# A transformer layer pair in fp32 on one core: the third branch's projection in chunk order ahead of its gates, weights through three staging buffers, four buffers handed to expert weights

## The chip, the core and the metric

The kernel runs on one core of a Trainium2 chip. The metric is the device time of one launch in microseconds; lower is better. Before the change it is 2053.32 us, the median of three runs.

## What is computed

Two blocks in fp32 on 256 tokens of width 1024. The part that the change touches is the end of the first block's mixer and the beginning of its mixture of experts:

```python
merged = (jax.nn.sigmoid(ga) * (o_a @ w_branch_a)
          + jax.nn.sigmoid(gb) * (o_b @ w_branch_b)
          + jax.nn.sigmoid(gc) * (o_c @ w_branch_c))   # gc, ga, gb: 1024 columns of h @ w_in
x = x + gt1 * (merged @ w_out)
h2 = rmsnorm(x, norm2_g) * (1.0 + sc2) + sh2
x = x + gt2 * hier_moe(h2, rg_w, rg_b, re_w, re_b, e_gate, e_up, e_down)
```

`o_a` and `o_b` have 1024 columns, `o_c` has 2048, so `w_branch_c` is 2048 x 1024 (8 MB) and the others are half of that. The experts are 32, each with three matrices of 2 MB: 201 MB that are all read, since tokens choose their two experts by data. After the experts come the second block's feed-forward layers, a gated mixer and an attention.

## The kernel before

**Engines and staging.** TensorE (PE) multiplies in fp32 by splitting each weight into a rounded high part H and a remainder L: `three` (L650 to L653) issues H times high, H times low and L times high of the other operand. SyncE (SP) issues nearly all loads. A load of 1 MB goes into one of five raw buffers (`NR` = 5, tiles m_49 to m_53 in the order rows), and feeds two *pieces* of 1024 columns. ScalarE (ACT) rounds a piece to H (L1597), VectorE (DVE) subtracts to get L (L2304); both sit in one of four piece slots (`NH` = 4). So ACT may make the piece that is four further on only when PE has used the present one, and a raw buffer is free when DVE has made the L of its second piece. ACT, DVE and SP each keep the order of `plan`: whatever stands in between waits its turn, and what stands behind waits with it. `ahead(p)` on each of them works up to piece p + 3.

**Branches.** For A, B and C the code loops over four groups of 256 columns: the gate (`Cg0` and so on, 2 pieces, moving operand hT) and the projection (`Cw0`, for C 4 pieces of 8 row chunks by 128 columns, moving operand ocT, the turned `o_c`). A piece is 24 matmuls. PE accumulates in PSUM: kind "m" goes round banks 0 to 3, kind "s" round banks 4 to 7, and `take` waits until the bank's last contents have been read. ACT makes the sigmoid of the gate in the buffer `gs` (L1806), DVE multiplies it by the projection (L2560), GpSimd (POOL) adds the product to `mg` (L3351), and for the last step ACT rounds `mg` to mgT high (`mg_high`, L1820) and DVE makes its low part (`mg_low`, L2580). In C the projection of a group is taken out in two halves of 256 columns, each with its own product and sum.

**Output projection.** `w_out` (pieces of `wo`: 2 chunks of rows by 512 columns, for both halves of the tokens) reads mgT. Its pieces 0 and 1 are multiplied as they come; piece 2 is held until piece 3 is there, so PE waits for the L of piece 3 before it goes on with piece 2. DVE multiplies by gt1 and adds to x (L3156, L3159), then comes the router, which ends in the logits `lg`, and the gather of tokens for the experts.

**Where expert weights go.** Each 1 MB half of an expert matrix has a place in a table (`by_half` in `plan_experts`): the raw buffers, places `ex` 0 to 10 and `pre` 0 to 6, which are stretches of memory that earlier tensors use. SP fetches into a place as soon as its last reader is done; this is written by hand in `sync` (L3432 and L3518 on): `ex` 0 to 4, 9 and 10 and `pre` 4 during branch C, `pre` 1, 0, 2 and the raw buffers around its end, `ex` 5 to 8 as `w_out` gives up the piece slots, and `pre` 5, 6 and 3 when the logits are complete. From then on a place is filled again when the experts' matmuls (L1115, L1126) have read it. `pre` 5 is the memory of the first half of ocT high (35360 on), `pre` 1 that of the first half of ocT low (39456 on), `pre` 0 that of the 2048 columns from 37408. The scratch buffers `wos`, `rj` and `rF[0]` of `w_out` and the router lie in `pre` 5.

## Time and profile before

| | |
|---|---|
| median of 3 runs | 2053.32 us (2052.53 to 2053.99) |
| profiled execution, its own time | 2053.77 us |
| its span, first to last instruction | 2051.9 us |
| PE busy | 1908.7 us, 93% |
| DVE busy | 1133.1 us, 55% |
| ACT busy | 903.5 us, 44% |
| mean granted TensorE clock | 0.97 |
| HBM read | 500.07 MB, 244 GB/s over the span |

The page divides the span into 40 slices of 51.3 us. Times in the rows below are microseconds from the span's start. PEld is the loading of weights into TensorE, SPq the queue from which SyncE issues DMAs. In the timeline a row is: start, duration, engine, line, operation, result<-inputs, shapes, number of instructions merged, and in brackets the idle time before it and what ended it. Matmul durations overlap, so that a matmul's price is the distance of two starts.

### The profile page before, as it was taken

What the parts mean: (1) busy time and instruction counts of PE and PEld (TensorE: products, weight loads), DVE (VectorE), ACT (ScalarE), POOL (GpSimd) and SP (SyncE); (2) the same over time, 40 slices, a digit from 0 to 9 for tenths busy, and PEclk for the clock granted to TensorE, in tenths of its full rate; (3) what the DMA queues carried; (4) which work ended last, traced back from release to release, by engine and by line L of the source; (5) the groups of instructions that cost most, each with busy time, mean ns of one, the idle gap of its engine ahead of it and who ended that gap; (6) DMA issues with size and microseconds to landing.
All of it is one profiled execution on the core that took longest, in us unless ns stands there. A gap on an engine that the chain in (4) does not pass through costs nothing.

```text
span 2051.9 us, 30543 instructions
## 1 busy us (share of the span) xinstructions
PE 1908.7 (93%) x12777; PEld 1485.8 (72%) x12777; DVE 1133.1 (55%) x1523; ACT 903.5 (44%) x1289; POOL 118.8 (6%) x101
## 2 busy tenths in 40 slices
PE   9999999999999866766699999999999999999998
PEld 7899988889984211111178888888888888988887
DVE  3678876678542110101156666756667666756666
ACT  4655555544342100000045555545456554675544
POOL 0244331001000000000000000000000000000000
PEclk9999999999999988788899999999999999999999
DMA  9654546788899999999985755545554555525552
GB/s 349 211 159 153 164 145 226 231 269 283 288 354 410 424 426 425 426 425 424 421 290 192 243 190 184 166 164 175 192 188 163 186 190 192 174 85 172 188 185 83
DMA packets 241761, 503.51 MB, mean 245 GB/s; under 512 B 11457, under 2 KB 165714, under 8 KB 222418
## 3 DMA queue, kind: packets, MB, share of 16 engines
q1 hardware_dynamic: 240720, 500.70, 67.8%
q8 instruction: 103, 1.69, 0.3%
q10 hardware_dynamic: 898, 0.80, 0.1%
q14 instruction: 40, 0.33, 0.0%
HBM read 500.07 MB, written 1.07 MB: 244 GB/s over the span
## 4 chain that ended last, share of the span: by engine, by line
PE 73%; DMA 14%; DVE 7%; ACT 3%; issue 2%; SPq 1%; POOL 0%; ACTq 0%; DVEq 0%
PE bank L651 14%; PE bank L712 14%; PE bank L653 13%; PE bank L652 13%; PE bank L714 7%; DMA m<-in_expert_w_up 4%; DMA m<-in_expert_w_down 4%; DMA m<-in_expert_w_gate 4%; PE bank L1115 3%; DVE m L2304 2%; PE bank L1126 2%; ACT m L1597 1%; PE bank L996 1%; SPq L3414 1%; DMA m<-in_ffn_w_in 0%
## 5 line engine op out<-in xcount | busy, mean ns | idle before, releaser
L2304 DVE TENSOR_TENSOR m<-m,m 128x1024 fp32r<-128x1024 f32 x505 | 625.7, 1254 | 287.0 <-ACT m L1597 284.8
L651 PE MATMUL bank<-m,m 128*128 128x256 f32 (+1 forms) x1960 | 658.4, 336 | 6.6 <-DVE m L2304 3.0
L653 PE MATMUL bank<-m,m 128*128 128x256 f32 (+1 forms) x1960 | 645.6, 329 | 0.0
L652 PE MATMUL bank<-m,m 128*128 128x256 f32 (+1 forms) x1960 | 645.2, 329 | 0.0
L1597 ACT ACTIVATE m<-m 128x1024 fp32r<-128x1024 f32 x505 | 524.2, 1054 | 223.1 <-PE bank L653 203.9
L712 PE MATMUL bank<-m,m 128*128 128x512 f32 x1248 | 439.8, 394 | 0.0
L651 PEld LDWEIGHTS bank<-m,m 128*128 128x128 f32 x1960 | 368.6, 188 | 55.7 <-DVE m L2304 10.0
L653 PEld LDWEIGHTS bank<-m,m 128*128 128x128 f32 x1960 | 368.6, 188 | 36.5
L652 PEld LDWEIGHTS bank<-m,m 128*128 128x128 f32 x1960 | 368.9, 188 | 33.8 <-issue 1.2
L714 PE MATMUL bank<-m,m 128*128 128x256 f32 x1248 | 352.7, 283 | 0.0
L712 PEld LDWEIGHTS bank<-m,m 128*128 128x128 f32 x1248 | 234.4, 188 | 54.0
L714 PEld LDWEIGHTS bank<-m,m 128*128 128x128 f32 x1248 | 234.6, 188 | 1.6
L1115 PE MATMUL bank<-m,m 128*32 128x512 f32 x1024 | 163.7, 674 | 59.8 <-DMA m<-in_expert_w_gate 33.3
L1115 PEld LDWEIGHTS bank<-m,m 128*32 128x32 f32 x1024 | 39.7, 121 | 175.3 <-issue 85.6
L1948 ACT ACTIVATE m<-bank 128x256 f32<-128x256 f32 x156 | 59.2, 379 | 161.5 <-PE bank L714 161.5
L1126 PE MATMUL bank<-m,m 128*32 128x512 f32 x512 | 91.3, 679 | 36.6 <-DMA m<-in_expert_w_down 30.8
L2855 DVE TENSOR_TENSOR m<-bank,m 128x256 f32<-128x256 f32 x156 | 65.6, 422 | 59.6 <-ACT m L1948 54.9
L1126 PEld LDWEIGHTS bank<-m,m 128*32 128x32 f32 x512 | 19.2, 122 | 101.1 <-DMA m<-in_expert_w_down 56.5
L2730 DVE TENSOR_TENSOR m<-bank,m 128x512 f32<-128x512 f32 x16 | 10.3, 686 | 142.1 <-PE bank L1126 142.1
L2724 DVE SCALAR_TENSOR_TENSOR m<-bank,m,m 128x512 f32<-128x512 f32 x8 | 6.0, 750 | 118.3 <-PE bank L1115 118.3
L2751 DVE TENSOR_TENSOR m<-m,bank 128x512 f32<-128x512 f32 x32 | 21.3, 686 | 87.1 <-PE bank L1198 87.1
L1859 ACT ACTIVATE m<-bank 128x512 f32<-128x512 f32 x8 | 4.8, 597 | 133.0 <-PE bank L1115 133.0
(352 smaller groups left out, 1384.1 us busy)
## 6 DMA issues: line engine op xcount, KB each, us to landing
m<-in_ffn_w_in SPq DMA_DIRECT2D x88, 1024.0 KB, 5.1
m<-in_w_in SPq DMA_DIRECT2D x60, 1024.0 KB, 5.2
m<-in_ffn_w_out SPq DMA_DIRECT2D x44, 1024.0 KB, 5.0
m<-in_expert_w_up SPq DMA_DIRECT2D x40, 1024.0 KB, 21.8
m<-in_expert_w_down SPq DMA_DIRECT2D x34, 1024.0 KB, 18.0
m<-in_expert_w_gate SPq DMA_DIRECT2D x33, 1024.0 KB, 22.8
m<-in_expert_w_gate SPq DMA_DIRECT2D x15, 2048.0 KB, 23.4
m<-in_expert_w_down SPq DMA_DIRECT2D x13, 2048.0 KB, 17.9
```

What stands on the lines that cost most here:

```text
L651: e.matmul(o, s[0], m[0], start=first, stop=False, skip_group_check=skip)
L652: e.matmul(o, s[0], m[1], start=False, stop=False, skip_group_check=skip)
L653: return e.matmul(o, s[1], m[0], start=False, stop=last, skip_group_check=skip)
L712: e.matmul(b[:, :].rearrange("p (h n) -> p h n", h=2), H, N.both[:, k], start=k == 0, stop=False, skip_group_check=True)
L714: ins = e.matmul(b[:, 0:256], L, N.T[0][:, k, :], start=False, stop=k == 7, skip_group_check=True)
L1115: ins = e.matmul(b[32 * j:32 * j + 32, :], XG(q, q + 1)[:, 0, k, 32 * j:32 * j + 32], block(ld, i), start=k == 0, stop=k == 7, skip_group_ ...
L1126: ins = e.matmul(b[n][32 * j:32 * j + 32, :], eT[q % 2][:, 128 * c + 32 * j:128 * c + 32 * j + 32], ld.raw[:, 1024 * i + 512 * n:1024 * i ...
L1597: inc(e.activation(rv(fit(q.H, q.view.shape)), q.view, ACT.Copy), "h", skey(q, "H"))
L1948: inc(e.activation(fb[6][:, 256 * b:256 * b + 256], k[:, 256:512], ACT.Copy), "ffn", (f"f{z}c", n, c, b))
L2304: inc(e.tensor_tensor(rv(fit(q.L, q.view.shape)), q.view, fit(q.H, q.view.shape), ALU.subtract), "l", skey(q, "L"))
L2751: taken(e.tensor_tensor(o, o if q else x[:, t, 512 * n:512 * n + 512], b[:, :], ALU.add), "ey", q, t, n, also=[("y", q, t, n)])
L2855: taken(e.tensor_tensor(o, k[:, 0:256], fb[6][:, 256 * b:256 * b + 256], ALU.add), f"f{n}{z}{c}", b, also=[(f"f{z}a", n, c, b)])
```

## The change

It touches branch C and its surroundings in each engine's program; what is computed stays the same.

1. The projection of C no longer goes group by group. `plan_third` takes `w_branch_c` in loads of 4 row chunks by 512 columns, first all columns of rows 0 to 511, then the next 512 rows, and so on, into four banks (0 to 3), one for each group of 256 columns. Seven of its eight loads (`Ca`, 14 pieces) come first, then the four gates (8 pieces, in banks 4 to 7), then the last load (`Cz`, 2 pieces, groups 2 and 3).
2. From branch C on, up to the end of `w_out`, weights go round three raw buffers (m_51, m_52, m_53). The other two (m_49, m_50) take expert weights when B's last weights have been split.
3. `pre` 5 and `pre` 1 are fetched when piece 7 of `Ca` is used (the first eight chunks of ocT are then read). `wos`, `rj` and `rF[0]` move by 2048 columns into `pre` 0, which is now fetched with `pre` 6 and 3 after the logits.
4. `gs` has two buffers for C (the second is B's). Products and sums are made over 512 columns at a time, once a group. `mg_high` and `mg_low` of groups 0 and 1 stand ahead of `Cz`, those of 2 and 3 behind it.

```diff
@@ -213,13 +213,13 @@
         plan, G = [], {}
         tails, counts = {}, {}
         loads, XL, OL = [], {}, {}
+        ring = list(range(NR))
 
         def load(dst, src, slot=None, release=None):
             if slot is None:
-                kind, n = "raw", NR
-                c = counts.get(kind, 0)
-                counts[kind] = c + 1
-                slot = (kind, c % n)
+                c = counts.get("raw", 0)
+                counts["raw"] = c + 1
+                slot = ("raw", ring[c % len(ring)])
...
+        def plan_third(gcol, W):
+            G["Ca"], G["Cz"] = [], []
+            for k0 in (0, 4, 8, 12):
+                for h in range(2):
+                    last = k0 == 12 and h == 1
+                    for i in range(4 if last else 0):
+                        plan_gemm2(f"Cg{i}", win, 8, [gcol + 256 * i])
+                    ld = load(lambda r: r.rearrange("p (k n) -> p k n", n=512),
+                              W[128 * k0:128 * k0 + 512, 512 * h:512 * h + 512].rearrange("(k p) n -> p k n", p=128))
+                    v = ld.raw.rearrange("p (k n) -> p k n", n=512)
+                    for i in range(2):
+                        G["Cz" if last else "Ca"].append(Piece(plan, ld, v[:, :, 256 * i:256 * i + 256], 1024, name="Cw",
+                                                               g=2 * h + i, k=k0, m=4, end=k0 == 12))
...
+        ring[:] = [(counts["raw"] + i) % NR for i in range(3)]
+        counts["raw"] = 0
+        plan_third(GC, a["w_branch_c"][0])
         plan_gemm1("wo", a["w_out"][0], 8, 0, 1024)
         plan_experts()
         plan_overflow()
-        counts["raw"] = 0
+        ring[:], counts["raw"] = range(NR), 0
...
-        gs = {"A": mem(37152, 512), "B": mem(44064, 512), "C": mem(43552, 512)}
+        gs = {"A": mem(37152, 512), "B": mem(44064, 512), "C": [mem(43552, 512), mem(44064, 512)]}
-        wos = mem(36384, 512)
-        rj = mem(36896, 512)
-        rF = [v256(mem(o, 1024)) for o in (35360, 44576)]
+        wos = mem(38432, 512)
+        rj = mem(38944, 512)
+        rF = [v256(mem(o, 1024)) for o in (37408, 44576)]
...
+            def products(name):
+
+                for p in walk(name):
+                    w.wait_ge(*skey(p, "L"))
+                    o = take(p.g, "Cw", p.g) if p.k == 0 else bank[p.g]
+                    for b in range(2):
+                        for i in range(4):
+                            k = p.k + i
+                            w.wait_ge("ocT", k // 2)
+                            ins = three(o[:, 256 * b:256 * b + 256], parts(p, 256 * i + 128 * b, 128),
+                                        (ocT[0][:, k, :], ocT[1][:, k, :]), k == 0 and b == 0, k == 15, True)
+                    used(ins, p, *([("Cw", p.g)] if p.end else []))
+
+            def third_branch():
+                products("Ca")
+                for i in range(4):
+                    if i == 1:
+                        router_bias()
+                    gemm2(f"Cg{i}", hT, h_ready, at="s")
+                    if i < 2:
                         ada_sum(10 + i)
+                products("Cz")
+                turn["m"] = 0
...
+            def third_branch():
+                run("Ca")
+                for i in range(4):
+                    def ev_gate(p):
+                        b = got(p.name, p.g)
+                        if i >= 2:
+                            w.wait_ge("bs", "C", i - 2)
+                        elif i:
+                            w.wait_ge("bs", "B", 3)
+                        else:
+                            w.wait_ge("full", ("ada", 5))
+                        taken(e.activation(gs["C"][i % 2], b[:, :], ACT.Sigmoid), p.name, p.g, also=[("bg_s", "C", i)])
+                    run(f"Cg{i}", ev_gate)
+                e.activation(eps[:, 2:3], eps[:, 0:1], ACT.Sqrt)
+                mg_high(0)
+                mg_high(1)
+                run("Cz")
+                mg_high(2)
+                mg_high(3)
...
+            def third_branch():
+                def ev_out(i):
+                    b = got("Cw", i)
+                    s = gs["C"][i % 2]
+                    w.wait_ge("bg_s", "C", i)
+                    taken(e.tensor_tensor(s, s, b[:, :], ALU.mult), "Cw", i, also=[("bsv", "C", i)])
+                for n, p in enumerate(walk("Ca")):
+                    if n == 4:
                         router_weights()
-                    run(f"{name}g{i}")
-                    if name == "C" and i == 3:
-                        for j in range(3):
-                            mg_low(j)
-                    run(f"{name}w{i}", ev_out)
-                    if name != "C":
-                        run_ada(*adas[name][i])
-                    elif i < 2:
+                for i in range(4):
+                    run(f"Cg{i}")
+                    if i < 2:
+                        ev_out(i)
                         ada_out(10 + i)
-                    if name == "C" and i == 2:
+                    if i == 1:
                         b = got("rbias")
                         taken(e.tensor_tensor(rt["bias"], b[:, 0:36], rB, ALU.add), "rbias")
+                mg_low(0)
+                mg_low(1)
+                run("Cz", lambda p: ev_out(p.g))
+                mg_low(2)
+                mg_low(3)
...
+            def third_branch():
+                for n, p in enumerate(G["Ca"]):
+                    ahead(p)
+                    if n == 2:
                         w.wait_ge("full", ("ocT", 7))
                         w.wait_ge(*skey(G["Bw3"][-1], "used"))
-                        for slot in ((0, 1), (2, 3))[i]:
+                        w.wait_ge("taken", ("cd", 3))
+                        for slot in (0, 1):
                             fetch(first("ex", slot))
-                        if i == 0:
-                            w.wait_ge("taken", ("cd", 3))
-                            fetch(first("ex", 4))
+                    if n == 5:
+                        for slot in (2, 3):
+                            fetch(first("ex", slot))
+                    if n == 8:
+                        fetch(first("ex", 4))
+                    if n == 10:
+                        w.wait_ge(*skey(G["Ca"][7], "used"))
+                        for slot in (5, 1):
+                            fetch(first("pre", slot))
+                run("Cg0", "Cg1")
+                w.wait_ge("taken", ("rbias",))
+                fetch(first("ex", 10))
+                run("Cg2", "Cg3")
+                w.wait_ge(*skey(G["Cg3"][-1], "used"))
+                fetch(first("pre", 4))
+                run("Cz")
...
-            w.wait_ge(*skey(G["Cw3"][-1], "used"))
-            for i in (0, 2):
-                fetch(first("pre", i))
+            w.wait_ge(*skey(G["Cz"][-1], "used"))
+            fetch(first("pre", 2))
...
-            for i in (5, 6, 3):
+            for i in (6, 0, 3):
```

Three places show how the order of instructions moves. Names like m_51 are buffers. The first is SyncE's queue from the first load of `w_out` to the first refill of an expert place. Before:

```order
L3414 DMA m_53<-in_w_out 128x4x512 [waits dve_l]
...
L3414 DMA m_82<-in_expert_w_up 128x2048 [waits used]
L3414 DMA m_49<-in_expert_w_up 128x2048 [waits dve_l]
L3414 DMA m_81<-in_expert_w_up 128x2048 [waits used]
L3414 DMA m_83<-in_expert_w_up 128x2048
L3414 DMA m_50<-in_expert_w_up 128x2048 [waits dve_l]
L3414 DMA m_51<-in_expert_w_down 128x2048 [waits dve_l]
L3414 DMA m_78<-in_expert_w_down 128x2048 [waits used]
...
L3414 DMA m_86<-in_expert_w_gate 128x2048 [waits full4]
L3412 DMA m_87<-in_expert_w_gate 128x1024
...
L3414 DMA m_84<-in_expert_w_up 128x2048
L3414 DMA m_68<-in_expert_w_down 128x2048 [waits ex_used]
```

After:

```order
L3463 DMA m_51<-in_w_out 128x4x512 [waits dve_l]
...
L3463 DMA m_52<-in_expert_w_down 128x2048 [waits dve_l]
L3463 DMA m_83<-in_expert_w_up 128x2048 [waits used]
L3463 DMA m_53<-in_expert_w_down 128x2048 [waits dve_l]
L3463 DMA m_51<-in_expert_w_down 128x2048 [waits dve_l]
L3463 DMA m_78<-in_expert_w_down 128x2048 [waits used]
...
L3461 DMA m_87<-in_expert_w_gate 128x1024 [waits full4]
...
L3463 DMA m_81<-in_expert_w_up 128x2048
L3463 DMA m_84<-in_expert_w_up 128x2048
L3463 DMA m_68<-in_expert_w_down 128x2048 [waits ex_used]
```

Four loads of expert weights (into m_49, m_50, m_82 = `pre` 1 and m_86 = `pre` 5) have moved up to a place ahead of the first load of `w_out`; m_81 = `pre` 0 has moved back to the place that `pre` 5 had. In all, from the first load of branch C to the one before the last `m_51<-in_expert_w_down`, there are 30 loads of 1 MB in either order.

The second is TensorE's queue where branch B ends and C begins. Before:

```order
L651 MATMUL bank0<-m133_181,m6_54 128x256
L652 MATMUL bank0<-m134_182,m6_54 128x256
L653 MATMUL bank0<-m133_181,m10_58 128x256
L651 MATMUL bank1<-m83_131,m7_55 128x256 [waits bank1_act,dve_l]
L652 MATMUL bank1<-m84_132,m7_55 128x256
```

After:

```order
L667 MATMUL bank0<-m134_182,m6_54 128x256
L668 MATMUL bank0<-m135_183,m6_54 128x256
L669 MATMUL bank0<-m134_182,m10_58 128x256
L667 MATMUL bank0<-m137_185,m7_55 128x256 [waits bank0_dve,dve_l]
L668 MATMUL bank0<-m138_186,m7_55 128x256
```

The last projection of B is in bank 0. What follows it went to bank 1 before; now it goes to bank 0 and waits for DVE's read of it (`bank0_dve`).

The third is VectorE's queue around the last pieces of branch C. m139/m140 is mgT low, m132 and m133 are `gs` of C, lines L2304/L2351 the subtractions of weights. Before:

```order
L2580 TENSOR_TENSOR m139_187<-m124_172,m138_186 128x512 [waits act_split] x3
...
L2304 TENSOR_TENSOR m12_60<-m5_53,m8_56 128x1024 [waits used,act_h]
L2560 TENSOR_TENSOR m132_180<-m132_180,bank3 128x256 [waits bank2_act,used]
L2304 TENSOR_TENSOR m13_61<-m1_49,m9_57 128x1024 [waits act_h]
L2560 TENSOR_TENSOR m132_180<-m132_180,bank0 128x256 [waits used]
L2580 TENSOR_TENSOR m139_187<-m124_172,m138_186 128x512 [waits act_split]
L2304 TENSOR_TENSOR m10_58<-m1_49,m6_54 128x1024 [waits act_h]
```

After:

```order
L2635 TENSOR_TENSOR m140_188<-m124_172,m139_187 128x512 [waits act_split] x2
L2351 TENSOR_TENSOR m12_60<-m3_51,m8_56 128x1024 [waits used,act_h]
L2613 TENSOR_TENSOR m132_180<-m132_180,bank2 128x512 [waits bank7_act,used]
L2351 TENSOR_TENSOR m13_61<-m4_52,m9_57 128x1024 [waits act_h]
L2613 TENSOR_TENSOR m133_181<-m133_181,bank3 128x512 [waits bank4_act,used]
L2635 TENSOR_TENSOR m140_188<-m124_172,m139_187 128x512 [waits act_split] x2
L2351 TENSOR_TENSOR m10_58<-m4_52,m6_54 128x1024 [waits act_h]
```

The last row of each is the L of `w_out`'s piece 3. Ahead of it stand now two products of 512 columns and two of `mg_low`, where two products of 256 and one `mg_low` stood.

## Rows read from the trace of the kernel before

**Rows 1.** The page: span, and GB/s in 40 slices of it

```profile
span 2051.9 us, 30543 instructions
...
GB/s 349 211 159 153 164 145 226 231 269 283 288 354 410 424 426 425 426 425 424 421 290 192 243 190 184 166 164 175 192 188 163 186 190 192 174 85 172 188 185 83
```

**Rows 2.** Stretches: us, busy PE, PEld, DVE, ACT, POOL, PEclk, DMA share, GB/s

```profile
585.00:595.00 10.00, 10.00 (x45) 8.10 (x44) 6.25 (x7) 4.09 (x7) 0.00 (x0) 1.00 0.96 404
595.00:597.00 2.00, 2.00 (x15) 1.74 (x14) 0.02 (x1) 0.94 (x2) 0.00 (x0) 1.00 0.47 82
597.00:605.00 8.00, 7.63 (x130) 6.16 (x129) 2.92 (x5) 2.95 (x8) 0.00 (x0) 1.00 0.99 394
605.00:616.00 11.00, 10.33 (x154) 7.18 (x153) 4.58 (x27) 5.04 (x5) 0.00 (x0) 1.00 1.02 410
616.00:620.00 4.00, 4.00 (x40) 2.45 (x42) 1.26 (x6) 2.21 (x5) 0.00 (x0) 1.00 0.85 310
...
660.00:1060.00 400.00, 284.38 (x1569) 88.50 (x1562) 53.53 (x80) 31.60 (x58) 0.00 (x0) 0.85 1.01 420
```

**Rows 3.** Timeline of SyncE's queue, 570 to 620 us

```profile
576.05 11.08 SPq L3414 DMA_DIRECT2D m<-in_expert_w_up  x5
595.04 7.82 SPq L3414 DMA_DIRECT2D m<-in_expert_w_down  x5
...
615.80 0.33 SPq L3414 DMA_DIRECT2D m<-in_expert_w_down  x1
```

**Rows 4.** Timeline of TensorE, end of branch B and beginning of C

```profile
507.61 0.28 PE L653 MATMUL bank<-m,m 128*128 128x256 f32 x1
507.73 0.28 PE L651 MATMUL bank<-m,m 128*128 128x256 f32 x1
```

**Rows 5.** Timeline of VectorE, the product of B's last group

```profile
507.93 0.69 DVE L2560 TENSOR_TENSOR m<-m,bank 128x512 f32<-128x512 f32 x1 [1.75 <-PE bank L653]
```

**Rows 6.** Timeline of ScalarE, last gate and last pieces of branch C

```profile
567.50 0.60 ACT L1806 ACTIVATE m<-bank 128x512 f32<-128x512 f32 x1 [1.73 <-PE bank L653]
...
569.52 1.66 ACT L1820 ACTIVATE m<-m 128x512 fp32r<-128x512 f32 x3
571.08 3.17 ACT L1597 ACTIVATE m<-m 128x1024 fp32r<-128x1024 f32 x3
576.11 1.06 ACT L1597 ACTIVATE m<-m 128x1024 fp32r<-128x1024 f32 x1 [1.85 <-PE bank L653]
580.16 0.63 ACT L1820 ACTIVATE m<-m 128x512 fp32r<-128x512 f32 x1 [2.99 <-POOL m L3351]
```

**Rows 7.** Timeline of VectorE, end of branch C

```profile
576.04 0.42 DVE L2560 TENSOR_TENSOR m<-m,bank 128x256 f32<-128x256 f32 x1 [0.39 <-PE bank L653]
...
578.89 0.42 DVE L2560 TENSOR_TENSOR m<-m,bank 128x256 f32<-128x256 f32 x1 [0.47 <-PE bank L653]
580.83 0.69 DVE L2580 TENSOR_TENSOR m<-m,m 128x512 fp32r<-128x512 f32 x1 [1.51 <-ACT m L1820]
581.78 2.36 DVE L2304 TENSOR_TENSOR m<-m,m 128x1024 fp32r<-128x1024 f32 x2 [0.26 <-ACT m L1597]
```

**Rows 8.** Timeline of TensorE, first matmul of `w_out` and of its piece 2

```profile
578.70 0.39 PE L651 MATMUL bank<-m,m 128*128 128x512 f32 x1
...
584.27 0.39 PE L651 MATMUL bank<-m,m 128*128 128x512 f32 x1
```

**Rows 9.** Timeline of GpSimd: sums over 512 columns in B, 256 in C

```profile
472.32 1.30 POOL L3351 TENSOR_TENSOR m<-m,m 128x512 f32<-128x512 f32 x1 [120.73 <-DVE m L2560]
485.91 2.20 POOL L3351 TENSOR_TENSOR m<-m,m 128x512 f32<-128x512 f32 x1 [12.29 <-DVE m L2560]
...
579.39 0.73 POOL L3351 TENSOR_TENSOR m<-m,m 128x256 f32<-128x256 f32 x1 [2.11 <-DVE m L2560]
```

**Rows 10.** Timeline of VectorE around the second of these sums

```profile
485.75 3.44 DVE L2304 TENSOR_TENSOR m<-m,m 128x1024 fp32r<-128x1024 f32 x2
```

**Rows 11.** Loads of w_branch_c: issue to landing

```profile
DMA to landing us min/median/max: 5.2/7.0/10.0
```

More of the change, by code:

```diff
@@ L579, in build @@
         rt["pr"] = tmp(64).rearrange("p (t e g) -> p t g e", t=2, g=4)
-        adas = {"A": later[4:8], "B": later[12:16], "C": []}
+        adas = {"A": later[4:8], "B": later[12:16]}
         def reach(p):
@@ L1520, in tensor @@
             ticks.join()
-            branch("C", ocT, lambda k: ("ocT", k // 2), 16)
+            third_branch()
             w_out()
@@ L1803, in ev_gate @@
                             w.wait_ge("oaL", 1)
-                        elif name == "C":
-                            w.wait_ge("full", ("ada", 5))
                         taken(e.activation(gs[name], b[:, :], ACT.Sigmoid), p.name, p.g, also=[("bg_s", name, i)])
                     run(f"{name}g{i}", ev_gate)
-                    if name == "C" and i == 3:
-                        e.activation(eps[:, 2:3], eps[:, 0:1], ACT.Sqrt)
-                        for j in range(3):
-                            mg_high(j)
                     run(f"{name}w{i}")
-                    if name != "C":
-                        run(("ada", *adas[name][i]))
+                    run(("ada", *adas[name][i]))
+            def third_branch():
[17 more added lines that the diff above has]
+                mg_high(3)
             def mg_high(j):
                 w.wait_ge(*skey(G["Cg3"][-1], "used"))
-                w.wait_ge("mg", "C", j, 1)
+                w.wait_ge("mg", "C", j, 0)
                 o = slice(512 * j, 512 * j + 512)
@@ L2172, in scalar @@
             ticks.join()
-            branch("C")
-            mg_high(3)
+            third_branch()
             def x_copy(g, t):
@@ L2547, in ev_out @@
                     def ev_out(p):
[L2548 to L2552 removed]
+                        b = got(p.name, 0)
+                        s = gs[name]
                         w.wait_ge("bg_s", name, i)
@@ L3147, in vector @@
             ticks.join()
-            branch("C")
-            mg_low(3)
+            third_branch()
             def ev_wo(p):
@@ L3434, in branch @@
                     run(f"{name}g{i}")
-                    if name == "C" and i == 3:
-                        w.wait_ge("taken", ("rbias",))
-                        fetch(first("ex", 10))
-                        w.wait_ge(*skey(G["Cg3"][-1], "used"))
-                        fetch(first("pre", 4))
-                        for p in G["Cw3"][:3]:
-                            ahead(p)
-                        w.wait_ge(*skey(G["Cw3"][1], "used"))
-                        fetch(first("pre", 1))
                     run(f"{name}w{i}")
-                    if name != "C":
-                        run(("ada", *adas[name][i]))
+                    run(("ada", *adas[name][i]))
                     if name == "A" and i == 1:
@@ L3517, in sync @@
             branch("B")
-            branch("C")
+            third_branch()
             ahead(G["wo"][0])
-            w.wait_ge(*skey(G["Cw3"][-1], "used"))
-            for i in (0, 2):
-                fetch(first("pre", i))
+            w.wait_ge(*skey(G["Cz"][-1], "used"))
+            fetch(first("pre", 2))
             run("wo")
```

39 lines of the change are left out of this document (11 added, 28 removed).

## Prediction

> **What bounds the kernel now.** I read the page first, then stretches around the end of the first block, then the timelines of the engines there. The page's row of bytes [rows 1] has a plateau of 410 to 426 GB/s from the 13th slice to the 20th, from 616 us to 1026; before it the rate is 145 to 354. The long stretch 660 to 1060 says the same: the DMA engines are busy all the time (share 1.01) at 420 GB/s, while PE has work for 284 of 400 us [rows 2]. So the experts are bound by loads, and what lies ahead of them is bound by PE: in 585 to 597 it is busy in every microsecond [rows 2], and the matmuls of branch C follow each other at 0.12 us [rows 4].
>
> The change is meant to load expert weights earlier, so the question is what the loads wait for where the plateau begins. From 585 to 595 the share is 0.96; then, in 595 to 597, it falls to 0.47 with 82 GB/s; from 597 on it is 0.99 and over 1 [rows 2]. SyncE's queue explains the hole: the five loads of `in_expert_w_down` begin to be issued at 595.04 [rows 3]. They wait for the piece slots and the raw buffer that `w_out` gives up, that is for PE. At that moment all earlier loads have landed, or the rate could not fall to 82. After the five come the three places that wait for the logits, and at 615.80 the first refill, which waits for the experts' first matmuls [rows 3].
>
> This gives the rule I forecast by: **what has been moved by 595, and when PE gets there, set the end of the experts.** In the two orders of SyncE's queue, 30 loads of 1 MB stand between the start of branch C and that hole, before and after; behind it stand the same waits, with `pre` 0 where `pre` 5 was. Four expert loads go earlier, but the loads that they overtake were in by 595 too. Nothing is gained: the DMA engines will only be busier before 585 and idle longer before 595. What is left is the path of PE.
>
> **The change on PE's path.** Its work stays: 24 pieces of 24 matmuls of one shape, two sums for the modulation, one for the router's bias. A piece takes 578.89 - 576.04 = 2.85 us, the distance of the two products that wait for the ends of two pieces [rows 7]. Cost 0.
>
> *Loads through three buffers.* A raw buffer is free when the L of its second piece, p, is made, and this begins when PE has used piece p - 4. The next load in the buffer holds piece p + 5, and ACT may begin on that when PE has used p + 1. Between the two ends lie 5 pieces, 14.2 us. H and L take about 2.6 us of them before the issue (1.06 + 1.22 and what separates them [rows 6, 7]); 11.6 us are left until the split would be late. PE would be late about 6 us after that: it has three more pieces, 8.5 us, less 2.3 for H and L. Landing took 5.2 to 10.0 us for these loads [rows 11]. Two expert loads may now stand ahead, each 1.05 MB at 420 GB/s = 2.5 us [rows 2], so up to 15 us. That is below 11.6 + 6.2 = 17.8. I take 0; the cover is this lead, and without it each late load costs its excess.
>
> *A wait at the start of C.* PE's order shows that the first piece of `Ca` writes bank 0, in which B's last projection has just been finished, and waits for DVE to read it. Before, the next bank was free and PE went on from 507.61 to 507.73 [rows 4]. The read runs from 507.93 for 0.69 us, to 508.62 [rows 5]. An engine follows another's end in about 0.05 us (POOL's sum ends at 580.12, ACT starts at 580.16, ends at 580.79, and DVE starts at 580.83 [rows 6, 7, 9]). So PE goes on at 508.67: **0.94 us lost**. Bounds 0.9 and 1.1; there is no other work for PE, whose queue keeps its order.
>
> *A wait in w_out.* I write W for `w_out`'s first matmul, 578.70 before; its piece 2 starts at W + 5.57 [rows 8]. PE needs the L of piece 3 by then. Before it was made at 581.78 + 1.22 = 583.00, W + 4.3, 1.3 us early (the pair took 2.36, and one subtraction takes 1.22) [rows 7]. After the change the gates end later: there are two pieces between the last gate and W, where there were four. So, in order:
> - ACT's last sigmoid moves from 567.50 to two pieces later, W - 5.50. As before it takes 2.02 us until `mg_high` and 0.52 for each of now two: ACT is free at W - 2.44 [rows 6]. Two roundings of 1.06 follow. DVE subtracts (`wo` 1) from W - 1.34 to - 0.12, so its product of group 2, ready since W - 2.66, is late: W - 0.20 to 0.49. Then comes the subtraction for `wo` 2, 0.40 to 1.62, and the product of group 3, 1.54 to 2.23.
> - POOL's sum over 512 columns took 1.30 us where DVE ran no subtraction, 2.20 where it began in one; that pair of subtractions then took 3.44 instead of 2.36 [rows 7, 9, 10]. Group 2's sum begins in a subtraction: 0.57 to 2.77. Group 3's does not: 2.81 to 4.11.
> - `mg_high` of group 3 starts at W + 4.15. From its start to the end of L of piece 3 it was 583.00 - 580.16 = 2.84 [rows 6, 7], so L ends at W + 6.99 and PE goes on at 7.04: **1.5 us lost**.
>
> Bounds for the second: both sums at 1.30 give W + 6.55, 1.0 us; both at 2.20 give 7.95, 2.4 us. I take the middle since each sum is nearest to its own row of the two.
>
> On the second and third of these steps the Trainium skill has a rule, "SBUF — State Buffer", section "Who interferes with whom": a DVE instruction with two SBUF inputs and a GpSimd instruction that reads SBUF hold a shared read port exclusively, and the second fully blocks. By that rule, which the 3.44 us bear out, the 0.9 us are waiting for the subtraction and not slower adding, so group 3's sum costs 1.30 and the loss is 1.5; if sums next to any DVE work cost 2.20, it is 2.4.
>
> *Everything behind* hangs on PE: the L of `wo`'s pieces 4 and 5 are needed only 5.6 us later, the last five loads, the logits, the refill. The hole at 595 opens later by the whole sum, and behind it the plateau has the same bytes to move. `mg_low` and products over 512 instead of 256 columns hide in DVE's idle time (0.39 to 1.51 us ahead of each row [rows 7]) but for what is counted. The scratch that moved into `pre` 0 costs nothing: `pre` 0 is filled in the third of the loads after the logits, and is read only for the second half of the first experts' matrices.
>
> **Sum:** 0.94 + 1.5 = 2.4 us later. The profiled execution would go from 2053.77 to 2056.2; it stood 0.45 above the median, so against the median it is 2053.3 + 2.4 = **2055.8 us**, rounded up, 0.12% slower. A measurement of this kernel tells about 0.2%, 4.1 us, from no change: this is within it.
>
> **The rivals.**
> - *The two waits are hidden.* If DVE's order or POOL's timing is kinder than I walk it, the time stays at 2053 to 2054.5. For it: the second wait has 1.3 us of slack before. Against it: the bank wait is plain in the order. Chance 0.13.
> - *The ring starves PE*, the one that ends on the other side. Its place is the loads of `Ca` and of the gates behind the pairs `ex` 0/1, 2/3 and `pre` 5/1. It decides from landings over 17.8 us after the freeing. With 10.0 us for a landing and each pair 5 us, it needs 3 us more, from SyncE being held up at one of its hand-written waits. Each of three places would then cost one expert load, 2.5 us: 7.5 us on top, 2063. One such place gives 2058.3. Chance 0.13 for over 2057.4, with the bound of 2.4 us and other late splits among them.
> - *Early loads pay.* If some of the plateau's idle time is really owed to these four loads (the share is 0.85 in 616 to 620 [rows 2]), they take up to 4 x 2.5 = 10 us off: 2045.8. Against it stand the hole at 595 and the equal counts. The Trainium skill, "DMA: Bandwidth & Descriptors", section "Rules for kernel authors", advises to issue the DMA early and wait on it late; by it the change is right, but the rows say that the queue ran dry after these loads anyway. Chance 0.04.
> - *It does not do what it says*: a raw place is released as late as before. The order shows m_49 and m_50 filled ahead of `w_out`, so I give it nothing of its own.
>
> **How the numbers follow.** My case has 0.70 and spans 2054.8 to 2057.3 (bounds 0.9 + 1.0 and 1.1 + 2.4, and half a microsecond of scatter). Down to 2053.0 and up to 2058.6, the range takes in most of the hidden case and one starved load, and leaves out some 0.15. Faster by over 0.2% (below 2049.2): 0.04. Slower by over 0.2% (above 2057.4): 0.14. The rest, 0.82, is the same.
>
> **What would show it.** After the change: PE idle for about 0.9 us before `Ca`, put down to DVE's product; PE idle about 1.5 us inside `w_out`, put down to DVE's subtraction; GB/s higher in 500 to 560 and a share well under 0.96 before the hole, with the five loads issued about 2.4 us later than 595.04; the plateau as long as before, its end 2.4 us later. I am wrong if the queue is still loaded when these five are issued, or if PE waits in branch C.

## The result and the profile after

The changed kernel took 2055.77 us (median of 20 runs, 2053.80 to 2056.95). The kernel before, run beside it, took 2052.68 us (20 runs, 2051.39 to 2053.99). The ratio is 1.0014, with a 95% interval of 1.0008 to 1.0020: slower by 3.1 us, inside the 0.2% that the prediction called "the same", and within its range. The profiled execution took 2055.20 us, with a span of 2053.4. Of all runs in this document one is left out, of the kernel called *one held* below: it took 3694.9 us.

The page of the changed kernel, span and GB/s in 40 slices (to set beside [rows 1]):

```profile
span 2053.4 us, 30540 instructions
...
GB/s 349 210 163 149 165 144 227 232 270 280 327 295 413 425 427 423 427 424 425 420 302 188 243 190 185 168 164 172 193 190 164 186 188 192 175 86 172 187 184 83
```

Stretches of it: us, busy PE, PEld, DVE, ACT, POOL, PEclk, DMA share, GB/s (to set beside [rows 2], moved by the delay):

```profile
500.00:560.00 60.00, 59.13 (x546) 58.15 (x544) 32.73 (x35) 22.52 (x23) 3.49 (x2) 1.00 0.91 327
560.00:585.00 25.00, 25.00 (x188) 23.61 (x187) 14.20 (x16) 12.36 (x17) 4.73 (x3) 1.00 0.71 251
585.00:589.00 4.00, 2.77 (x13) 1.97 (x12) 3.74 (x4) 2.59 (x3) 0.00 (x0) 1.00 0.26 39
589.00:593.00 4.00, 4.00 (x19) 3.25 (x18) 0.55 (x2) 1.15 (x2) 0.00 (x0) 1.00 1.00 424
597.00:599.00 2.00, 2.00 (x14) 1.69 (x13) 0.89 (x1) 0.58 (x3) 0.00 (x0) 1.00 0.19 29
599.00:605.00 6.00, 6.00 (x31) 4.91 (x29) 1.45 (x3) 1.74 (x4) 0.00 (x0) 1.00 0.96 370
...
660.00:1060.00 400.00, 286.90 (x1568) 88.66 (x1568) 53.83 (x81) 30.91 (x55) 0.00 (x0) 0.83 1.01 421
```

Two of the same stretches of the kernel before:

```profile
500.00:560.00 60.00, 60.00 (x554) 58.72 (x553) 34.31 (x40) 24.04 (x25) 5.69 (x6) 1.00 0.86 297
560.00:585.00 25.00, 25.00 (x187) 23.82 (x187) 14.71 (x17) 13.04 (x17) 2.40 (x4) 1.00 0.81 299
```

The early loads do come early: from 500 to 560 the rate rises from 297 to 327 GB/s. It is paid back from 560 to 585 (299 to 251), and just before the last loads of this stage the queue now runs dry at 585 to 589 (39 GB/s); the kernel before had a shallower place of this kind a little earlier, 123 GB/s at 582 to 585. The hole is still there: 29 GB/s at 597 to 599, in place of 82 at 595 to 597. From 660 to 1060 the plateau is as before, 421 GB/s. SyncE's queue, timeline (to set beside [rows 3]):

```profile
586.99 0.34 SPq L3463 DMA_DIRECT2D m<-in_expert_w_down  x1
587.37 0.43 SPq L3463 DMA_DIRECT2D m<-in_expert_w_up  x1
589.25 16.49 SPq L3463 DMA_DIRECT2D m<-in_expert_w_down  x6
...
618.68 0.33 SPq L3463 DMA_DIRECT2D m<-in_expert_w_down  x1
```

The row of six merges two things: a load for a raw buffer at 589.25, and the five loads that stood at 595.04 before, which are issued from 597.92 on. The first refill is issued at 618.68 where it was 615.80. Both are 2.9 us later, by the profile's own zero.

Where PE lost it, timeline of TensorE: the starts of branch C and of `w_out`'s piece 2 (to set beside [rows 4, 8]):

```profile
507.37 0.28 PE L669 MATMUL bank<-m,m 128*128 128x256 f32 x1
508.52 0.36 PE L667 MATMUL bank<-m,m 128*128 128x256 f32 x1 [0.87 <-DVE m L2603]
508.71 0.28 PE L668 MATMUL bank<-m,m 128*128 128x256 f32 x1
...
580.09 0.39 PE L667 MATMUL bank<-m,m 128*128 128x512 f32 x1
...
585.43 0.40 PE L669 MATMUL bank<-m,m 128*128 128x512 f32 x1
587.06 0.47 PE L667 MATMUL bank<-m,m 128*128 128x512 f32 x1 [1.23 <-DVE m L2351]
587.37 0.39 PE L668 MATMUL bank<-m,m 128*128 128x512 f32 x1
```

VectorE, timeline: B's last product, then the products of groups 2 and 3 with a subtraction of weights between them, `mg_low` twice, and three subtractions, the first of which makes the L of `w_out`'s piece 3 (to set beside [rows 5, 7]):

```profile
507.68 0.69 DVE L2603 TENSOR_TENSOR m<-m,bank 128x512 f32<-128x512 f32 x1 [1.76 <-PE bank L669]
...
579.87 0.68 DVE L2613 TENSOR_TENSOR m<-m,bank 128x512 f32<-128x512 f32 x1
580.46 1.22 DVE L2351 TENSOR_TENSOR m<-m,m 128x1024 fp32r<-128x1024 f32 x1
581.60 0.68 DVE L2613 TENSOR_TENSOR m<-m,bank 128x512 f32<-128x512 f32 x1
583.53 1.95 DVE L2635 TENSOR_TENSOR m<-m,m 128x512 fp32r<-128x512 f32 x2 [1.25 <-ACT m L1868]
585.73 3.50 DVE L2351 TENSOR_TENSOR m<-m,m 128x1024 fp32r<-128x1024 f32 x3 [0.26 <-ACT m L1632]
```

GpSimd and then ScalarE, timeline: the sums of groups 2 and 3 into `mg`, `mg_high` twice, and the roundings behind (to set beside [rows 6, 9]):

```profile
580.63 3.46 POOL L3404 TENSOR_TENSOR m<-m,m 128x512 f32<-128x512 f32 x2 [15.62 <-DVE m L2613]
```

```profile
582.86 0.63 ACT L1868 ACTIVATE m<-m 128x512 fp32r<-128x512 f32 x1 [3.22 <-POOL m L3404]
584.11 0.64 ACT L1868 ACTIVATE m<-m 128x512 fp32r<-128x512 f32 x1 [0.62 <-POOL m L3404]
584.65 2.94 ACT L1632 ACTIVATE m<-m 128x1024 fp32r<-128x1024 f32 x3
```

With W = 580.09 the walk of the prediction can be laid beside the rows: product of group 2 at W - 0.22 (foreseen - 0.20), product of group 3 at W + 1.51 (1.54), the sums from W + 0.54 to 4.00 (0.57 to 4.11), `mg_high` of group 3 at W + 4.02 (4.15), L of piece 3 done at 585.73 + 1.22, W + 6.86 (6.99).

### The profile page after: what moved, and what is told of

Its sections match the earlier page's. It is cut to its first block, busy times and chain, and to the rows that moved or that the text cites. A ratio compares the mean times of both kernels' runs of the same rounds, so it can differ in the third digit from the quotient of the medians.

```text
span 2053.4 us, 30540 instructions
## 1 busy us (share of the span) xinstructions
PE 1911.3 (93%) x12777; PEld 1487.0 (72%) x12777; DVE 1134.2 (55%) x1519; ACT 903.3 (44%) x1289; POOL 119.1 (6%) x97
## 3 DMA queue, kind: packets, MB, share of 16 engines
q8 instruction: 103, 1.69, 0.3%
## 4 chain that ended last, share of the span: by engine, by line
PE 75%; DMA 11%; DVE 7%; ACT 3%; issue 2%; SPq 1%; POOL 0%; ACTq 0%; DVEq 0%
PE bank L667 14%; PE bank L728 13%; PE bank L669 13%; PE bank L668 13%; PE bank L730 7%; DMA m<-in_expert_w_down 5%; DMA m<-in_expert_w_up 4%; PE bank L1150 3%; DMA m<-in_expert_w_gate 3%; PE bank L1161 2%; DVE m L2351 2%; PE bank L1031 1%; ACT m L1632 1%; SPq L3463 1%; DVE m L2469 0%
## 5 line engine op out<-in xcount | busy, mean ns | idle before, releaser
L2351 DVE TENSOR_TENSOR m<-m,m 128x1024 fp32r<-128x1024 f32 x505 | 627.3, 1257 | 291.0 <-ACT m L1632 288.9
```

The costliest lines, as they stand in the source:

```text
L2351: inc(e.tensor_tensor(rv(fit(q.L, q.view.shape)), q.view, fit(q.H, q.view.shape), ALU.subtract), "l", skey(q, "L"))
```

## Three stretches to measure by

The times of 11 runs leave an interval of about 0.0009 of 2053 us, 1.8 us, to either side. That is too wide to tell 1 us from 0. The distances in the trace vary less, if two things that differ from one execution to the next are left out: where in the span branch C begins (506.75 to 507.93 in the profiles of this study), and the experts' stretch behind. So each kernel is read by three rows: **P**, VectorE's product of B's last group (as [rows 5]); **W**, `w_out`'s first matmul (as [rows 8]); **R**, the first refill in SyncE's queue (as [rows 3]). P to W is branch C, W to R is `w_out` and the path to the experts. For the kernel before they are 507.93, 578.70, 615.80; changed 507.68, 580.09, 618.68.

| kernel | P to W | W to R | P to R, against before | median less the median of before, us | ratio, 95% interval |
|---|---|---|---|---|---|
| before | 70.77 | 37.10 | | | |
| changed | 72.41 | 38.59 | +3.13 | +3.09 | 1.0008 to 1.0020 |
| changed, again | 71.90 | 38.64 | +2.67 | +3.38 | 1.0006 to 1.0025 |
| bank turned | 70.78 | 38.58 | +1.49 | +1.69 | 0.9998 to 1.0016 |
| split first | 72.40 | 37.31 | +1.84 | +2.00 | 1.0002 to 1.0020 |
| both | 70.78 | 37.30 | +0.21 | +0.83 | 0.9993 to 1.0011 |
| both, again | 70.96 | 37.26 | +0.35 | +0.67 | 0.9995 to 1.0012 |
| wait in before | 71.88 | 37.11 | +1.12 | +1.50 | 0.9999 to 1.0018 |
| late four | 71.89 | 38.64 | +2.66 | +3.18 | 1.0008 to 1.0026 |
| ring of five | 71.90 | 38.64 | +2.67 | +3.56 | 1.0008 to 1.0026 |
| ring of two | 71.89 | 38.95 | +2.97 | +3.01 | 1.0004 to 1.0022 |
| one held | 71.87 | 38.60 | +2.60 | +4.35 | 1.0012 to 1.0029 |
| both and half | 70.78 | 37.30 | +0.21 | -0.92 | 0.9989 to 1.0007 |
| both and half, again | 70.96 | 37.26 | +0.35 | -0.15 | 0.9991 to 1.0008 |

The theory to test is the prediction's: PE lost its time at two waits, and neither the three buffers nor the early loads cost or gain anything. Its rivals: the three buffers or their transfers cost the time; or the early loads pay and hide a larger loss. One thing more was to be settled: in the changed kernel's profile P to W was 1.64 longer, and the bank wait explains 1.1 of it. The rest is a cadence, by which I mean the mean distance of two matmuls' starts: from 508 to 555 PE's matmuls of 256 columns started 120.0 ns apart (means over each 5 us of the timeline), everywhere around it 118.7.

## The experiments

**The changed kernel again**, as yardstick.

> The changed kernel once more, as the yardstick of the runs beside it. All theories: 2.5 to 3.5 us over the kernel before (2055.2 to 2056.2 if that one runs at 2052.7).

2056.19 us, 3.4 over the kernel before. Its branch C was half a microsecond shorter, 71.90, and the cadence was 118.7 throughout. So the 0.5 us of the first profile come and go in the same kernel.

**The projection in other banks.**

```diff
-                    o = take(p.g, "Cw", p.g) if p.k == 0 else bank[p.g]
+                    o = take((p.g + 1) % 4, "Cw", p.g) if p.k == 0 else bank[(p.g + 1) % 4]
...
-                turn["m"] = 0
+                turn["m"] = 1
```

> The projection's four sums stand in the banks 1, 2, 3, 0 in place of 0, 1, 2, 3, so that the first one no longer meets the bank that VectorE has yet to read. Theory of TensorE's path: the gap of 1.15 us ahead of the branch shrinks to 0.12, which gives back 1.0 us against the changed kernel. On the slower cadence (120.0 ns a matmul in the first part of the branch, 118.7 elsewhere) the two explanations part: if the stall sets it, the 120.0 goes with the stall, another 0.5 us, 1.5 in all; if the chunk order itself (its banks, weights or the split ahead) sets it, it stays, and only 1.0 is gained. Theory that the lost time is the three staging buffers' or the transfers': no gain from this, 0.0, since the loads stay as they are.

2054.50 us. TensorE's timeline, the same seam:

```profile
507.61 0.28 PE L669 MATMUL bank<-m,m 128*128 128x256 f32 x1
507.72 0.28 PE L667 MATMUL bank<-m,m 128*128 128x256 f32 x1
```

The gap is gone and P to W is back at 70.78. Against the second profile of the changed kernel, with the same cadence, that is 1.12 us; W to R is unchanged. The median fell 1.7 us against the changed kernel beside it; that is 0.6 more than the trace explains, and less than the interval of 1.8 us.

**The split of `w_out`'s piece 3 ahead of the last slices** of the merged activations. On ScalarE and on VectorE, before `mg_high(2)` and before `mg_low(2)`:

```diff
+                ahead_to(G["wo"][0].j + NH)
```

> ScalarE and VectorE make the halves of w_out's third piece ahead of the last two slices of the merged activations, not behind them; nothing else changes. Theory of TensorE's path: the gap of 1.63 us inside w_out is what VectorE's late half causes, so it goes and 1.2 to 1.4 us come back, unless the group of w_out that wants the last slices comes so early that they are late now: then less than 0.7. Theory of the three buffers or the transfers: 0.0. Theory that the early expert loads pay and cover a larger loss: 1.4 or more.

2054.81 us. TensorE's timeline at the start of `w_out`'s piece 2:

```profile
584.84 0.40 PE L669 MATMUL bank<-m,m 128*128 128x512 f32 x1
585.18 0.47 PE L667 MATMUL bank<-m,m 128*128 128x512 f32 x1
```

W to R falls from 38.59 and 38.64 to 37.31, by 1.3 us; 0.2 of the 1.5 stay. They stand in the same place: the step into piece 2 is 0.34 where it was 0.23 in the kernel before, and the next matmul starts 0.31 later and not 0.23. This profile has the slow cadence in branch C again (72.40), which is why P to R stands at +1.84. VectorE's timeline, then GpSimd's, show what the sums cost now:

```profile
581.61 1.72 DVE L2352 TENSOR_TENSOR m<-m,m 128x1024 fp32r<-128x1024 f32 x1
```

```profile
580.04 4.44 POOL L3406 TENSOR_TENSOR m<-m,m 128x512 f32<-128x512 f32 x2 [15.61 <-DVE m L2614]
```

With one more subtraction beside the second sum, the two sums take 4.44 us in place of 3.46, and the subtraction 1.72 in place of 1.22. It does no harm, since `mg_high` of group 3 is now needed last.

**Both edits**, run twice.

> The two edits together. Theory of TensorE's path: the gains add up, 2.4 us without the cadence and 2.9 with it, so the kernel stands within 0.5 us of the kernel before (2052.3 to 2053.3 against 2052.7), although its three staging buffers and early expert loads are those of the changed kernel. Theory of the three buffers or the transfers: it stays 2 to 3 us over the kernel before. Theory that the early loads pay: it falls more than 1 us below the kernel before.

> The two edits together, once more beside the next kernel. Theory of TensorE's path: 2.4 to 2.9 us under the changed kernel, 2052.5 to 2053.7, and within 0.8 us of the kernel before.

2053.64 and 2053.88 us, 0.8 and 0.7 over the kernel before, within the interval of no difference. Against the changed kernel the first is 2.6 us lower, as expected; 0.8 over the kernel before is more than the 0.5 that the first expectation allowed, and 2053.88 is 0.2 above the second's bound. P to R is +0.21 and +0.35 (in the second, with matmuls of 120.0 ns from 560 to 580). The gains add up in P to R, with three buffers and early loads in place. The rival that blames buffers or transfers said 2 to 3 us over the kernel before, and the one in which early loads pay said more than 1 us under it; neither came.

**The bank wait alone, in the kernel before.**

```diff
             ticks.join()
+            turn["m"] -= 1
             branch("C", ocT, lambda k: ("ocT", k // 2), 16)
```

> The kernel before with one thing more: the branch's first product goes to the bank that VectorE has not read yet, as in the change; order and buffers are those of before. Theory of TensorE's path: a gap of 1.1 us where there was 0.12, so 1.0 us slower than the kernel before. On the cadence: if the stall sets it, matmuls from there to the next change of shape (the small product for the adaptive weights at about 525) run at 120.0 in place of 118.7 ns, about 0.2 us more; if the chunk order sets it, 118.7 all through. If the wait were hidden: 0.0.

TensorE's timeline, the same seam:

```profile
506.43 0.28 PE L653 MATMUL bank<-m,m 128*128 128x256 f32 x1
507.58 0.36 PE L651 MATMUL bank<-m,m 128*128 128x256 f32 x1 [0.87 <-DVE m L2561]
507.77 0.28 PE L652 MATMUL bank<-m,m 128*128 128x256 f32 x1
```

2054.33 us, P to W 71.88: the wait costs 1.11 us, the same as in the changed kernel, and W to R stays at 37.11. The rows say how 1.11 comes about. The gap is 1.15 where it was 0.12, 1.03 more, and the matmul behind the first one starts 0.19 later and not 0.12. The cadence after this wait was 118.7.

**Four early loads late again.** In SyncE's queue the two raw places are filled behind the fetch of `ex` 10, which waits for the router's bias, and `pre` 5 and 1 with `pre` 4 behind `Cg3`. (The expectation counts five; `pre` 4 stood there already, so four have moved.)

```diff
                     if q.load.final is q and q.load.succ and q.load.succ.n not in fetched:
+                        if q.j < G["Ca"][0].j and q.load.succ.release:
+                            held.append(q.load.succ)
+                            fetched.add(q.load.succ.n)
+                            continue
                         fetch(q.load.succ)
...
                     if n == 10:
                         w.wait_ge(*skey(G["Ca"][7], "used"))
-                        for slot in (5, 1):
-                            fetch(first("pre", slot))
+                        pass
...
                 fetch(first("ex", 10))
+                for ld in held:
+                    fetch(ld)
...
-                fetch(first("pre", 4))
+                for slot in (4, 5, 1):
+                    fetch(first("pre", slot))
```

> The changed kernel with five of its early expert loads (two into staging buffers, three into the experts' own) issued late, after the second gate of the branch and after the fourth; all else as changed. Theory that the early loads gain nothing because all of them are in before the queue drains: as the changed kernel, within 0.3 us, with the same stretch of plateau after the first refill. Theory that the early loads pay: 1 us or more slower than the changed kernel. Theory that they do harm beside the branch (a load in the way of another, or the slower cadence of 120.0 ns from the heavier traffic between 500 and 560): 0.5 us or more faster, with a cadence of 118.7.

Stretches of this kernel, columns as above:

```profile
500.00:560.00 60.00, 59.13 (x549) 58.15 (x549) 32.59 (x35) 23.12 (x23) 3.48 (x2) 1.00 0.73 257
560.00:585.00 25.00, 24.65 (x180) 22.77 (x178) 14.58 (x17) 12.93 (x17) 4.74 (x3) 1.00 0.93 364
```

The rate of 500 to 560 falls from 327 to 257 GB/s: 70 GB/s over 60 us are 4.2 MB, four loads. The time is 2056.01 us, P to R +2.66, both as in the changed kernel, and the last load of an expert weight is issued 407.5 us after the first refill, in the changed kernel's two profiles 406.5 and 407.3. So taking these four loads early neither gains nor harms. That the cadence was 118.7 here says nothing of their traffic, since the changed kernel, run again, had 118.7 with that traffic.

**Five staging buffers, and two.**

```diff
-        ring[:] = [(counts["raw"] + i) % NR for i in range(3)]
+        ring[:] = [(counts["raw"] + i) % NR for i in range(NR)]
```

and `range(2)` for two.

> The branch's weights go round five staging buffers again, the new order stays, and the first expert loads into the two buffers more come late. Theory of TensorE's path: as the changed kernel, within 0.3 us. Theory of the three buffers: 1.5 to 3 us faster, the gap inside w_out smaller, since pieces come earlier. Theory that early loads pay: 1 us or more slower.

> The branch's weights go round two staging buffers in place of three. Theory of TensorE's path, by the buffer's cycle: a piece's buffer comes free one piece earlier than its use allows for, the load takes 5.2 to 10.0 us, and the lead of 11.6 us of three buffers falls by a third or more; at 7.8 us or less some loads come late and VectorE and ScalarE with them, TensorE waits 0 to 8 us in the branch, and the kernel is 0 to 8 us slower than the changed one. Theory that three buffers already cost 1.5 us or more: two cost at least twice that. 0.0 to 0.3 means the ring is wide enough even at two.

2056.39 and 2056.22 us. With five, both stretches are those of three to 0.01, and the median, 3.6 over the kernel before, lies 0.2 to 0.5 above the changed kernel's two, within the scatter. The rival of the three buffers said 1.5 to 3 us faster, the one of early loads 1 us or more slower. With two, P to W is unchanged, although the branch's last load is issued ten microseconds later; SyncE's timeline of the changed kernel, then of the ring of two:

```profile
551.46 0.38 SPq L3463 DMA_DIRECT2D m<-in_w_branch_c  x1
```

```profile
561.58 0.37 SPq L3463 DMA_DIRECT2D m<-in_w_branch_c  x1
```

Only `w_out` feels it: W to R is 0.3 longer, and PE's wait for VectorE inside `w_out` is 1.60 in place of 1.23. In branch C the only wait of PE in either kernel is the one for VectorE's product. The three buffers are wide enough, and so would two be, nearly.

**One load held over the hole.**

```diff
-                        for slot in (5, 1):
-                            fetch(first("pre", slot))
+                        fetch(first("pre", 5))
...
                 for kind in (5 + i, 7 + i):
                     fetch(first("ex", kind))
+            fetch(first("pre", 1))
```

> The changed kernel with one early expert load (1 MB into the experts' own buffer 1) taken over the drained stretch: issued behind the four loads that follow w_out, where before this change and with it it was in long before. Theory that what has been moved by the drained stretch sets the experts' end: 1 MB at the plateau's 420 GB/s is 2.5 us, so 2.0 to 3.0 us slower than the changed kernel, about 2058.5. Theory that only TensorE's arrival counts, the experts' loads having slack: 0.0. The kernel with five loads issued late but still ahead of the drained stretch ran as the changed one, so a loss here is the crossing, not the lateness.

The median is 2057.56 us, 4.4 over the kernel before, where the changed one is 3.1 to 3.4 over it: 1.0 to 1.3 us for 1 MB, not the 2.0 to 3.0 expected. That is less than the interval of 1.8 us of one set of runs. But five sets have the load ahead of the hole (changed, changed again, late four, ring of five, ring of two). The mean of this kernel less that of the kernel before beside it is 1.3 us above the average of the same difference over the five, with 0.8 to 1.8 as the 95% interval when the runs are resampled. Its P to R is unchanged, so the loss lies in the experts' loads. A second, shallow hole behind the first may account for the missing part. The stretch 614 to 632, in the changed kernel and then in this one:

```profile
614.00:632.00 18.00, 18.00 (x282) 7.99 (x280) 5.74 (x21) 5.09 (x9) 0.00 (x0) 1.00 1.00 399
```

```profile
614.00:632.00 18.00, 17.20 (x273) 7.12 (x272) 5.71 (x20) 5.09 (x9) 0.00 (x0) 1.00 1.02 420
```

Ahead of the first refills the queue of the changed kernel thins out: 21 GB/s short of 420 over 18 us are 0.38 MB, 0.9 us. The rate with the held load, 420 GB/s, is what filling it would give. So 1.6 us were to be expected; the 0.3 to 0.6 still missing lie within the scatter. That the second hole takes the 0.9 us is reckoned from the rates, and no run here tests it by itself.

**Both edits and half a load ahead of the hole**, run twice. The scratch `wos` and `rj` moves out of `pre` 0, and the upper half of `pre` 0 (0.5 MB) is loaded before `w_out` ends:

```diff
-        wos = mem(38432, 512)
-        rj = mem(38944, 512)
+        wos = mem(43552, 512)
+        rj = mem(44064, 512)
...
+                elif ld.slot == ("pre", 0):
+                    then_inc(e.dma_start(ld.raw[:, 0:1024], ld.src[:, 0:1024]), "ld_pre0", ("ld", ld.n), by=16)
...
             fetch(first("pre", 2))
+            ld = first("pre", 0)
+            then_inc(e.dma_start(ld.raw[:, 1024:2048], ld.src[:, 1024:2048]), "ld_pre0", by=16)
```

> The two edits together, and half a load (0.5 MB) of the expert buffer that overlaps the staging area of w_out issued some microseconds before the drained stretch at 595, the other half where it was. Theory that what has been moved when the queue drains sets the experts' end: 0.5 MB is 1.2 us of the plateau, so 0.6 to 1.2 us less than the kernel with the two edits alone, and about 1 us below the kernel before. Theory that TensorE's arrival alone counts: 0.0 against the two edits. Theory that early loads pay wherever they are: no statement on this half.

> The two edits and the half load ahead of the drained stretch, once more. Theory that what has been moved there sets the experts' end: 0.6 to 1.8 us under the two edits alone, and 0.3 to 1.2 us under the kernel before. Theory that the first reading was scatter: level with the two edits.

2051.91 and 2053.06 us: 1.7 and 0.8 below the two edits alone, 0.9 and 0.2 below the kernel before. P to R is that of the two edits, so what is gained is gained in the loads, as with one held and in the other direction. Reckoned in the same way from the means of both pairs together, the gain is 1.2 us, 0.7 to 1.8 when the runs are resampled. Two expectations missed: 1.7 is more than the 0.6 to 1.2 of the first, and 0.2 below the kernel before is less than the 0.3 to 1.2 of the second. The second hole seems to grow: 614 to 632 ran at 387 and 378 GB/s, against 391 and 402 with the two edits alone, which is clear in the second pair only. The intervals of this kernel against the kernel before both take in no difference: it is the best of these kernels by its medians, but not shown to beat the kernel before.

## Why the prediction was right, step by step

The two waits of PE are the mechanism that was forecast, and the experiments take each away and put the first one in. That the time, 2055.77 us, falls on the forecast 2055.8 is luck all the same. The forecast stood on 2053.3 us for the kernel before, and its twenty runs gave 2052.68; the change itself cost 3.1 us and not 2.4. The two misses cancel.

- **The rule** (what has been moved when PE reaches the hole sets the experts' end): right in direction, shown from both sides. Four loads moved without crossing the hole change nothing (late four), one held over it costs 1.3 us, half a load brought ahead of it gains 1.2, both by the means over several sets of runs. The price, 2.5 us for 1 MB, was too simple. The prediction read the share of 0.85 at 616 to 620 [rows 2] only as a rival's argument; it is a second hole, into which part of a late load may fit. That did not touch the sum, since the change moves no load over the first hole.
- **"Its work stays ... Cost 0"**: right. The slow cadence of the first profile made it look wrong by 0.5 us; the other profiles show that it comes and goes. Without the bank wait P to W is 70.78, and it was 70.77 before.
- **The ring, cost 0**: right, and with more room than reckoned, since even two buffers cost 0.3 us and put no wait into the branch. In hindsight the chance of 0.13 for a starved PE was high.
- **The wait at the start of C, 0.94 us**: the mechanism is right, the term was sized too low; it is 1.11. PE resumed at 508.52, 0.15 after the end of the read at 508.37. The prediction took 0.05 for that, from rows in which GpSimd, ScalarE and VectorE follow each other. The matmul behind the first one was late too, by 0.07. The experiment that turns the banks takes it away, the one that puts it into the kernel before adds it.
- **The wait in `w_out`, 1.5 us**: W to R is 1.49 and 1.54 longer. The gap itself is 1.63 instead of 0.23, 1.40; the slow first matmul behind it (0.31 to the next, not 0.23) gives the rest. Taking both sums at 2.20 would have given 2.4, both at 1.30 1.0; the rows show 3.46 for the pair, one of each, which is what the Trainium skill's rule of the shared port ("SBUF — State Buffer", "Who interferes with whom") says. Split first bears it out once more: as soon as a subtraction runs beside the second sum, that sum too costs 2.2 (4.44 for the pair).
- **The sum**, 2.4 us, was to be 1.11 + 1.5 = 2.6. The medians say 3.1 and 3.4, with an interval of 1.6 to 4.1 us for the first. What the remaining 0.5 to 0.8 us are, if they are more than scatter, is open; 0.7 to 0.8 also stay in the kernel with both edits, of which its P to R explains 0.2 to 0.35. The profiles do not place them: from R to the issue of the last expert load it is 408.0 us before, 406.5 and 407.3 in the changed kernel, 408.8 and 407.2 with both edits, a scatter larger than what is sought.
- Forecasts for the profile: PE idle before `Ca`, from VectorE's product, and inside `w_out`, from VectorE's subtraction, no wait in the branch, higher GB/s in 500 to 560, a queue that has run dry when the five loads are issued, and these later than 595.04. All came; the five loads are 2.9 us later where 2.4 was forecast. The end of the plateau was to come 2.4 us later. Reckoned from P, the last expert load is issued after 515.85 us in the kernel before and after 517.53 and 517.88 in the changed kernel's two profiles, 1.7 and 2.0 later.

## What to carry to other kernels

Ahead of a stage that is bound by loads, look for the place where the queue runs dry: here a load moved earlier gained only when it crossed that place. A second dry place behind it may give part of that back, or take part of a loss. When a block of work is rearranged, look at its two seams first: which bank the first product meets, and what the first consumer behind it stands behind on VectorE and ScalarE. Both losses here were seams, and an edit of two lines took away each of them nearly whole. For effects of one microsecond in two thousand, compare distances between named instructions over several profiles; one profile can carry half a microsecond that is not the kernel's.

## What the hardware showed beyond this

- **Two cadences of the same matmul.** Matmuls of 128x256 start on average 118.7 ns apart in most stretches and 120.0 in some, at a granted clock of 1.00 in both. The bank wait and the chunk order were the two explanations put forward. Of eight profiles with that wait the branch was slow from 508 to 555 or so in two (changed, split first), 0.5 us each; of six without it none was slow there. But without the wait the branch's last part, 560 to 580, was slow in two (both again, both and half again: 0.2 us each), and the changed kernel, run again, had 120.0 within 155 to 180 instead, long before the branch. So neither the stall nor the chunk order by itself sets it; what does is open.
- **A bank just read by VectorE** is written by PE 0.15 us after the end of the read (508.37 to 508.52 in the changed kernel), and the first matmul after that wait delays the next by another 0.07 us (0.19 between their starts, not 0.12).
